# Down projection as seven quarter products in a decoder's feed-forward block

## The reference

```
u = causal_depthwise_conv(h @ w_up, conv_w)      # h: 1024 x 1024, w_up: 1024 x 5632
gate, val = split(u)
f = (silu(gate) * val) @ w_down                  # 1024 x 2816 @ 2816 x 1024
x = x + rms_norm(f, g_post)                      # then, in layer 0, rms_norm for the next mixer
```

## Time and profile before

| what | value |
|---|---|
| median of 3 runs | 2688.99 us (2687.26 to 2690.5) |
| profiled execution | 2685.92 us, its span 2683.9 us |
| PE busy | 2599.2 us (97%) |
| VectorE busy | 1636.2 us (61%) |
| ScalarE busy | 1115.2 us (42%) |
| GpSimd busy | 1179.1 us (44%) |
| bytes over DMA | 238.07 MB, mean 89 GB/s |
| mean granted TensorE clock | 0.991 |

### The profile page before, as it was taken

One profiled execution on the slowest core, in us unless ns is written; L12 is line 12 of the kernel. 1 busy time (PEld: TensorE's weight loads), 2 busy tenths in 40 slices (PEclk: granted clock), 3 DMA queues, 4 the chain that ended last, 5 costly groups with the idle time before them and its releaser, 6 DMA issues. The chain is left out here.

```text
span 2683.9 us, 34327 instructions
## 1 busy us (share of the span) xinstructions
PE 2599.2 (97%) x12821; PEld 2156.9 (80%) x12821; DVE 1636.2 (61%) x1740; ACT 1115.2 (42%) x1645; POOL 1179.1 (44%) x721
## 2 busy tenths in 40 slices
PE   6999999999989999999999999999989999999998
PEld 5788888888778888888888688888878888888887
DVE  5677666676168666665455658557448666665454
ACT  6445545544443443433244334434533443433242
POOL 3444333434404778784443111111413877774442
PEclk9999999999999999999999999999999999999999
DMA  3111011111432222225554111012522222234553
GB/s 120 35 38 47 31 39 47 42 36 42 124 114 101 79 85 79 87 80 168 174 175 135 61 36 48 23 55 69 160 87 78 87 71 94 71 105 154 169 189 113
DMA packets 84541, 238.07 MB, mean 89 GB/s; under 512 B 8928, under 2 KB 22816, under 8 KB 84416
## 3 DMA queue, kind: packets, MB, share of 16 engines
q1 hardware_dynamic: 84416, 236.39, 26.6%
HBM read 189.66 MB, written 46.69 MB: 88 GB/s over the span
## 5 line engine op out<-in xcount | busy, mean ns | idle before, releaser
L391 POOL TENSOR_TENSOR f_wlo<-f_raw,f_whi 128x512 fp32r<-128x512 f32 (+1 forms) x210 | 426.5, 2032 | 499.4 <-ACT f_whi L432 499.4
L703 DVE TENSOR_TENSOR f_hlo<-f_hraw,f_hhi 128x512 fp32r<-128x512 f32 x88 | 182.1, 2075 | 200.9 <-ACT f_hhi L490 200.9
L432 ACT ACTIVATE f_whi<-f_raw 128x512 fp32r<-128x512 f32 (+1 forms) x210 | 171.9, 834 | 274.5 <-PE f_value L75 252.7
L391 POOL TENSOR_TENSOR f_wlo<-f_sums,f_whi 128x512 fp32r<-128x512 f32 x144 | 188.2, 1317 | 39.8 <-ACT f_whi L432 39.8
L432 ACT ACTIVATE f_whi<-f_sums 128x512 fp32r<-128x512 f32 x144 | 90.3, 627 | 270.7 <-POOL f_sums L397 270.7
L73 PE MATMUL f_value<-x_hi,f_whi 128*128 128x512 f32 x416 | 162.6, 391 | 1.6 <-POOL f_wlo L391 1.6
L74 PE MATMUL f_value<-x_lo,f_whi 128*128 128x512 f32 x416 | 162.6, 391 | 0.0
L75 PE MATMUL f_value<-x_hi,f_wlo 128*128 128x512 f32 x416 | 162.5, 391 | 0.0
L73 PE MATMUL f_part<-f_whi,f_hhi 128*128 128x512 f32 x352 | 137.9, 392 | 0.0
L75 PE MATMUL f_part<-f_whi,f_hlo 128*128 128x512 f32 x352 | 137.5, 391 | 0.0
L74 PE MATMUL f_part<-f_wlo,f_hhi 128*128 128x512 f32 x352 | 137.1, 389 | 0.0
(11 more groups left out here) (539 smaller groups left out, 7652.2 us busy)
## 6 DMA issues: line engine op xcount, KB each, us to landing
f_raw<-in_ffn_w_up SPq DMA_DIRECT2D x88, 512.0 KB, 3.6
f_raw<-in_ffn_w_down SPq DMA_DIRECT2D x88, 512.0 KB, 3.6
hidden<-f_hid SPq DMA_DIRECT2D x44, 512.0 KB, 2.8
f_hraw<-hidden SPq DMA_DIRECT2D x88, 256.0 KB, 3.9
g_raw_first<-in_gdn_w_in SPq DMA_DIRECT2D x16, 512.0 KB, 3.6
g_raw<-in_gdn_w_in SPq DMA_DIRECT2D x16, 512.0 KB, 4.2
f_xt<-x_mid SPq DMA_DIRECT2D x16, 512.0 KB, 4.8
l_raw_first<-in_gla_w_in SPq DMA_DIRECT2D x12, 512.0 KB, 3.6
```

The costliest lines, as they stand in the source:

```text
L391: pool.tensor_tensor(part_of(w_lo, k), source, part_of(w_hi, k).bitcast(F32), ALU.subtract) \
L432: act.activation(part_of(w_hi, k), source, ACT.Copy).then_inc(s_hi, 1)
L703: dve.tensor_tensor(h_lo[d % FFN_SLOTS][:, :], h_raw[d % HIDDEN_RAWS][:, :], plain32(h_hi[d % FFN_SLOTS][:, :]), ALU.subtract).then_inc(s_ ...
```

## The change

The down projection is made like the up projection, by quarter products. Inner tiles are taken in 11 pairs (`PAIRS`); with even and odd hidden tile, near and far tokens, each pair needs seven products of a 512-token operand and a 512-column operand instead of eight: 12 matmuls each, 77 steps. They run in four stages (0: plain operands, low columns; 1 and 2: sums of weights; 3: plain, high columns); within stages 0 to 2 the two products of a pair alternate (`first_ps` in the two `part` banks, `second_ps` in `gate` and `value`).

- Hidden operands: besides the four plain quarters, three sums of them a pair of tiles. DVE makes them in the up phase (`hidden_sum`, four 128 x 512 operations a pair of inner tiles, called in `products(p)` for even p), SP stores seven operands for each pair to DRAM, in place of one store per tile.
- Weight operands: `down_sums` on DVE makes two (stage 1) or three (stage 2) 512-column sums for each pair. Weight low parts are made by GpSimd in stage 0 (22 steps) and by DVE (`down_low`) in the other 55.
- Joins: results of stages are kept and joined by ACT (`keep_products`) and DVE (`first_quarter` ... `last_row`). The near token tiles (`lead_rows`) are complete after stage 2, the far ones (`acc`) after stage 3.
- The weight ring now has ten half slots, the hidden ring 4 slots (5 before), and the raw hidden ring 4 (3 before), placed in two regions. The last 4 steps are held back (12 matmuls a tile).
- GpSimd waits, before its first `combine`, until the first pair's fourth hidden sum is stored (its buffer is shared).
- The end work of all eight token tiles falls after stage 2: `m_deviation` writes its squares to `xn` and so waits for the store of x two tiles before; the first `store_x` comes after all loads.

```diff
+    steps = [(stage, *step) for stage in range(3)
+             for step in ((0, 0), *(x for k in range(1, PAIRS) for x in ((0, k), (1, k - 1))), (1, PAIRS - 1))]
+    steps += [(3, 0, k) for k in range(PAIRS)]
+    STEPS = len(steps)
+    HELD = STEPS - HIDDEN_SLOTS
+    BY_POOL = 2 * PAIRS
...
+        def hidden_sum(pair, n):
+
+            even, odd = hid[0], hid[1]
+            both = hidden_sums[min(pair, 1)]
+            dve.drain()
+            if n == 0:
+                if pair:
+                    dve.wait_ge(s_fstore, 16 * pair)
+                dve.tensor_tensor(both[:, 0, :], even[:, near], odd[:, near], ALU.add)
+            elif n == 1:
+                dve.tensor_tensor(both[:, 1, :], both[:, 0, :], even[:, far], ALU.subtract).then_inc(s_hsum, 1)
+                dve.tensor_tensor(even[:, near], even[:, far], even[:, near], ALU.subtract).then_inc(s_hsum, 1)
+            else:
+                dve.wait_ge(s_sstore, 16 * (pair + 1))
+                dve.tensor_tensor(both[:, 0, :], odd[:, far], both[:, 1, :], ALU.subtract).then_inc(s_hsum, 1)
...
             join(u2, p1, part_ps[0][:, far])
             if p > PLAIN:
                 activated(p - 1)
+            if p % 2 == 0:
+                hidden_sum(p // 2 - 1, 0)
             dve.drain()
             dve.wait_ge(s_prod, task(p, S3) + 1)
             join(u3, u2, part_ps[1][:, near])
+            if p % 2 == 0:
+                hidden_sum(p // 2 - 1, 1)
...
             conv(2 * p, gate_ps, gate, near_value)
+            if p % 2 == 0:
+                hidden_sum(p // 2 - 1, 2)
...
+        pool.wait_ge(s_fstore, 16)
         for pair in range(PLAIN, FT):
             operands(pair)
-        for d in range(STEPS):
-            low(FIRST_DOWN + d, raw[(2 * FT + d) % FFN_RAWS][:, :])
+        for d in range(BY_POOL):
+            low(FIRST_DOWN + d, down_source(d))
...
+        def down_low(d):
+            if BY_POOL <= d < STEPS:
+                dve.wait_ge(s_hi, FIRST_DOWN + d + 1)
+                k = FIRST_DOWN + d
+                dve.tensor_tensor(part_of(w_lo, k), down_source(d), plain32(part_of(w_hi, k)), ALU.subtract) \
+                    .then_inc(s_dlo, 1)
...
+            if stage == 1:
+                dve.tensor_tensor(first, e[:, high_cols], e[:, low_cols], ALU.subtract).then_inc(s_tsum, 1)
+                dve.drain()
+                dve.tensor_tensor(second, o[:, high_cols], first, ALU.subtract).then_inc(s_tsum, 1)
+                return
+            dve.tensor_tensor(first, o[:, high_cols], e[:, high_cols], ALU.subtract).then_inc(s_tsum, 1)
+            dve.drain()
+            dve.tensor_tensor(second, first, e[:, low_cols], ALU.add).then_inc(s_tsum, 1)
+            dve.drain()
+            dve.tensor_tensor(second, second, o[:, low_cols], ALU.subtract).then_inc(s_tsum, 1)
...
+        def lead_row(i):
+            dve.drain()
+            dve.wait_ge(*tile_done(2, 1, i))
+            x = lead_rows[i][:, low_cols]
+            quarter(lead_rows[i][:, high_cols], second_ps[i], acc[i][:, high_cols], ALU.add)
+            quarter(x, second_ps[i], x, ALU.add)
...
         def m_deviation(t):
...
+            act.wait_ge(s_mix, 16 + 2 * t + 2 if t < NT // 2 else 24 + t - NT // 2 + 1)
+            if t >= 2:
+                act.wait_ge(s_xout[t % 2], 16 * (t // 2))
+                if pre_gain is not None:
+                    act.wait_ge(s_xs, t - 1)
+            act.activation(xn[t % 2][:, :], m_of(t)[:, :], ACT.Square, accum_out=ss[:, t:t + 1])
...
+        for d in range(6 * PAIRS):
+            if d - 1 in joins:
+                joins[d - 1]()
+            down_low(d + 4)
+            hidden_low(d + 3)
+            down_sums(d + 5)
+            if d == 1:
+                hidden_sum(PAIRS - 1, 0)
+                hidden_sum(PAIRS - 1, 1)
+            elif d == 4:
+                hidden_sum(PAIRS - 1, 2)
```

More of the change, by code:

```diff
@@ new lines, in store_fourth @@
+        def store_fourth(pair):
+            sp.wait_ge(s_hsum, 3 * pair + 3)
+            sp.dma_start(hidden[pair, 6], hidden_sums[min(pair, 1)][:, 0, :]).then_inc(s_fstore, 16)
+        def load_hidden(d):
+            stage, second, k = steps[d]
+            if stage == 0:
+                sp.wait_ge(s_store[second], 16 * (k + 1))
+            elif stage == 1:
+                sp.wait_ge(s_sstore, 16 * (k + 1))
+                for i in range(2):
+                    sp.wait_ge(s_store[i], 16 * PAIRS)
+            elif stage == 3:
+                sp.wait_ge(s_fstore, 16 * (k + 1))
+                sp.wait_ge(*low_done(steps.index((2, 1, PAIRS - 1))))
@@ L328, in load_hidden @@
             if d >= HIDDEN_RAWS:
                 sp.wait_ge(s_hlo, d - HIDDEN_RAWS + 1)
-            elif PLAIN < FT:
+                if d < 2 * HIDDEN_RAWS:
+                    sp.wait_ge(s_prod, FIRST_DOWN)
+            else:
                 sp.wait_ge(s_lo, FIRST_DOWN)
-            sp.dma_start(h_raw[d % HIDDEN_RAWS][:, :], hidden[k, :, near if d < FT else far]) \
-                .then_inc(s_hraw[d % HIDDEN_RAWS], 16)
+            sp.dma_start(h_raw(d)[:, :], hidden[k, H_OPERAND[stage, second]]).then_inc(s_hraw[d % HIDDEN_RAWS], 16)
@@ L372, in _ @@
                     sp.dma_start(pre[:, :], pre_gain.partition_broadcast(P)).then_inc(s_gain, 16)
[L373 to L379, removed]
+            if d == 6 * PAIRS + HIDDEN_RAWS:
+                load_x(0)
+                load_x(1)
+        for t in range(NT):
+            if t == 1 and lead is not None:
+                sp.wait_ge(*low_done(STEPS - 1))
                 lead.load(sp)
@@ new lines, in high_hidden, with down_high @@
+            act.activation(h_hi[d % HIDDEN_SLOTS][:, :], h_raw(d)[:, :], ACT.Copy).then_inc(s_hhi, 1)
+        def down_high(d):
+            if d >= STEPS:
+                return
+            stage, second, k = steps[d]
+            if stage in (1, 2):
+                made = sums_made(stage, k)
+                act.wait_ge(s_tsum, made if not second else made - 1 if stage == 1 else made - 2)
+            else:
+                n = rows_of(stage, k)[1 if stage == 3 else second]
+                act.wait_ge(s_raw[n % FFN_RAWS], 16 * (n // FFN_RAWS) + 16)
+            copy(FIRST_DOWN + d, down_source(d))
@@ L706, in products, with last_row @@
+        def last_row(i):
+            dve.drain()
+            dve.wait_ge(s_m, i + 1)
+            x = acc[i][:, high_cols]
+            quarter(x, first_ps[i], x, ALU.add)
         def products(p):
```

461 lines of the change are left out of this document (271 added, 190 removed).

## The result

The changed kernel takes 2740.03 us (median of 4 runs, 2737.13 to 2742.81) for 2689.74 before: ratio 1.0188, 95% interval 1.0171 to 1.0206. The profiled execution's span is 2735.3 us for 2683.9, 51.4 us more. The forecast was 2721 in a range of 2676 to 2748: the sign and the mechanism of the up phase were right, and the change was put 19 us too small. The down phase came out 27 us dearer than forecast and the up phase with step 2's wait 5 us cheaper.

What follows compares the result with a forecast made beforehand. PE bounds the kernel now, with the DVE, POOL and ACT ring only 0.68 us a pair behind. Down phases −36.4 and up phases +68 give +32 on 2685.9, 2718, or 2721 as a median; range 2676 to 2748.

Steps and rivals of the forecast that it cites:

- The ring: Up phase: DVE, POOL and ACT form a loop with 0.68 us slack a pair; sums add 4.85 us an even pair.
- What would show it: List of expected signs: PE waits 3 to 4 us every second pair, sums 1.1 to 1.9 us, down phase 35 us later.
- the late start of GpSimd: Up phase: waiting for the first fourth sum holds POOL's first combine from 859.23 to about 869, costing 3 us a layer.
- The reserve at step 2: Down start: PE's 8 us reserve does not save it, since step 2 needs hidden_low(2) behind activated(21); 2 us lost.
- rival 1: Up phase: sums do not pay POOL's turn, 2.55 us an even pair; 2680 us in all, faster; chance 0.13.
- 66 x 2.71 = 179 us: Down phase: the first 66 steps keep PE's pace of 2.71 us each, 179 us a layer.
- The tails: End of down phase: 71 us in layer 0, with 7.0 us a tile, and 46.9 us in layer 1.
- rival 3: Down phase binds too, through late third-stage rows or DVE's lists in the last stage; about 2743 us; chance 0.17.
- the likeliest case: The forecast itself: sums pay POOL's turn, 2721 us, own range 2700 to 2738; chance 0.52.
- the DMA half: Rival 3's third-stage rows come late: 20 us of DMA in each layer at most.
- DMA at 0 us: Third stage of the down phase: loads need 290 GB/s against 331 GB/s while busy, so no cost was taken.
- Rivals 1, 2, 4 and 5: Total times: 2, sums hidden, 2657 (0.06); 4, turns fall better, 2689 to 2694 (0.10); 5, all PE saving, 2629 (0.02).

Runs made afterwards that it cites:

- the kernel whose only edit covers the 0.70 us: Changed kernel with hidden splits ahead of weight splits in the down loop, on ScalarE and VectorE: 2727.46 us (1.0140).
- unblocked sums: Changed kernel with one SBUF operand of each hidden sum of tile pairs 1 to 9 replaced by an idle PSUM half: 2699.17 us (1.0032).
- ScalarE's new order: Changed kernel with, in ScalarE's up phase, the first product's copy before all high parts and the scaled gate before the last: 2689.15 us (1.0000).
- the early gate: Changed kernel with only the scaled gate moved ahead of the last high part on ScalarE in the up phase: 2755.32 us (1.0255).
- the skew: Kernel with three reorderings and squares in idle buffers, plus VectorE's m_normed of tile t+1 ahead of x_normed of tile t: 2656.90 us (0.9887).

## Why the prediction was right, and where it was short

**The ring, right.** "Each even pair from 4 to 20, nine a layer, gets four DVE sums of two SBUF operands inside the ring ... That is 4.85 us an even pair." The four sums read 1.53, 0.84, 1.59 and 0.74 us, 4.7 in all; two of them lie under the 1.1 to 1.9 us that "What would show it" gave for each. That the turn and not the length is paid is shown from two sides (two columns: 1.09 us beside GpSimd and 0.16 beside none; PSUM operand: 0.69), and that the sums alone suffice for the loss by the kernel before with nothing of the change but them (+56). The forecast for the sums, 68 us with the late start of GpSimd, measured 63.0 (both up phases and both waits at step 2).

**The reserve at step 2, right in sum and wrong in make-up.** I counted a lag of 35 at pair 21 and 2 us lost at step 2. PE was 24 and 25 us late at the down start and lost 7.4 and 5.8 there: the reserve was used in the up phase and paid back at step 2. It is paid back even where the sums cost little, so rival 1's price ("−1") was too low too.

**66 x 2.71 = 179 us, the step that failed.** Measured without the wait at step 2: 191.0 (1254.76 to 1453.23, less 7.43) and 187.9 us. Most of the 12.0 and 8.9 us over it are two terms that were missing. First, the sentence "It slips under 0.1 us a pair of steps, against a lead of some 6 us": the slip is 0.12 when rows are there, but the eight joins at the stage's start, 5.05 us, which I had put nowhere, take most of the lead. The third stage took 8.0 and 5.7 us more than 59.6. That VectorE's list is the cause is shown by the kernel whose only edit covers the 0.70 us (60.1 us in both layers); how the 8.0 and 5.7 divide between the slip, the joins and the late rows is not. Second, about 2.4 us a layer in stage 0 are the clock, which the prediction did not count: after the wait at step 2 the granted clock was 0.50, the lower of the two levels (1.2 for 2.4 GHz), and step 2 took 5.1 us for 2.7 (4.9 in layer 1).
```profile
1265.00:1270.00 5.00, 2.18 (x5) 1.82 (x6) 4.83 (x6) 0.00 (x0) 2.17 (x1) 0.50 0.35 98
1270.00:1275.00 5.00, 5.00 (x18) 3.93 (x17) 1.68 (x3) 0.00 (x0) 0.00 (x0) 0.73 1.00 348
```
**The tails, nearly right.** Forecast 71 us to the phase's end, 72.6 to the next matmul as before's was 1.6 later; measured 76.3. Layer 1: 46.9, measured 49.2. The cycle of 7.0 us is there:
```profile
1486.31 0.17 DVE L937 RECIPROCAL f_rms<-f_std 128x1 f32<-128x1 f32 x1 [3.60 <-ACT f_std L610]
...
1493.38 0.16 DVE L937 RECIPROCAL f_rms<-f_std 128x1 f32<-128x1 f32 x1 [0.80 <-ACT f_std L610]
```
The 3.60 is the store of x row 1 behind the next mixer's load, which I had seen and priced lower; with the squares in idle buffers this wait reads 0.80.

**Which case it was.** The time is rival 3's, "the down phase binds too", and 2 us above the likeliest case's own range of 2700 to 2738. Of rival 3's two causes it was VectorE's list and not the queue; I gave it 0.17 and took the DMA half for its price. DMA at 0 us was right: with the list shortened, 256 KB rows came in time at the same sizes and counts. The four loads of a pair of steps, which one estimate put at 7.0 us (77 us a stage), then went through a stage of 60.1 us, 5.46 a pair. That answers the estimate; the 331 GB/s did not, since it is what the queue moved while busy and not over a stretch (255 to 259 GB/s in this stage). Rivals 1, 2, 4 and 5 are out, since the sums pay GpSimd's turn and stretch the ring. Rival 1's sum would not have held either: unblocked sums gave 2699 and not 2680, since the step-2 wait and the third stage were missing from it.

Left open: the 2.5 us by which the up phase of layer 0 is longer than before even with ScalarE's new order (432.3 for 429.8). Nearly all of it is one wait: PE stands 2.3 us for a value convolution in the last plain pair (at 876.87; at 871.58 in the changed kernel, and not at all before). There GpSimd's first combine comes late, at 866.31 for 859.23 (869 and 3 us were forecast), and its operations now fall beside the token sum ahead of that convolution, which takes 2.21 us for 1.23. No run takes the late start away, so that this is the cause is only argued. Open as well: the 15 us of the early gate, where the fourth sum's turn is shown and has the right size, but was not tried with that sum taken away.

## What to carry to other kernels

Work put on an engine that is 64% busy is not free if that engine stands in a ring with 0.7 us of slack: find the ring and the place in it that waits (here a copy queued behind an unrelated wait), because moving that one copy gave 42 us, as much as sums cut to two columns (42) or moved off the shared port (41), and keeps the output. A small VectorE instruction with both operands in SBUF can cost the rest of GpSimd's current instruction, however short it is itself (1.09 us for two columns here, 0.16 where GpSimd rested); put one operand in PSUM or lay it where GpSimd rests. And when a list is checked against a pace, count the one-off items at a stage's start too, since a list with no slack never makes them good. Mended so, by order alone, the seven products are worth 0.7% (0.9927), and 1.0% with the squares out of the stores' way (0.9904; 0.9887 with the skew, which is not told apart from it).

## What the hardware showed that I had not expected

- Two of the two-column sums took 1.08 and 1.09 us beside GpSimd (18 of each), against 0.16 for one that met no GpSimd operation and 0.69 for 512 columns with a PSUM operand: the price is the turn that an instruction meets, not its length.
- After PE's wait of 2.88 us at 1118.95 the granted clock reads 0.91 and 0.74 in the two slices of 5 us around it and 1.00 before and behind them; the second counts 19 matmuls for 24 in a full one. Waits of 3.19 and 2.73 us (1036.08, 1201.80) did the same, waits of 1.05, 1.25 and 2.05 us (1077.51, 1160.36, 994.30) left it at 1.00. In the up phase PE makes this good inside the ring's period: its next wait is the shorter, and the fourth products stay 41.4 us apart. Behind the wait at step 2 it is lost.
- The first mixer, the same code in all kernels, ended between 800.86 and 807.74 us in the profiled executions. That alone is a spread of about 0.25%, so differences of one or two us were read from single stages and not from the whole.
